# Two strided attention patterns taken as two lanes of tokens

## The reference

```python
for g, (window, dil) in enumerate(((128, 1), (512, 4), (2048, 16))):
    q, k, v = qkv[:, :, g, 0], qkv[:, :, g, 1], qkv[:, :, g, 2]
    o, lam = band_attention(to_strided(q, dil), to_strided(k, dil), to_strided(v, dil), window // dil)
    outs.append(from_strided(o, dil)); lams.append(from_strided(lam, dil))
alpha = softmax(stack(lams), axis=0)
y = sum(alpha[..., None] * stack(outs), axis=0)      # then y @ w_out
```

## Time and profile before

| | |
|---|---|
| runs | 1695.08, 1688.87, 1686.69 us (median 1688.87) |
| the profiled execution, first to last instruction | 1693.3 us, 21693 instructions |
| TensorE busy | 1643.5 us (97%) |
| VectorE / ScalarE busy | 638.1 us (38%) / 452.3 us (27%) |
| chain that ended last | TensorE 76%, VectorE 12%, DMA 5%, ScalarE 4% of the span |
| mean granted TensorE clock | 0.990 of full speed |

### The profile page before, as it was taken

The page is one execution under the profiler, slowest core; times in us unless marked ns, Lnnn a source line. Parts: engine busy times, 40 slices in busy tenths (PEclk is TensorE's granted clock), DMA queues, the critical chain, the costliest instruction groups (busy, mean ns, idle before and its releaser), DMA issues.

```text
span 1693.3 us, 21693 instructions
## 1 busy us (share of the span) xinstructions
PE 1643.5 (97%) x8195; PEld 963.5 (57%) x8195; DVE 638.1 (38%) x1382; ACT 452.3 (27%) x1167; POOL 135.3 (8%) x280
## 2 busy tenths in 40 slices
PE   8999989999999999999999999989999999999997
PEld 7888777644344344435878868856743443444342
DVE  3689983422222222214033544554422222222223
ACT  3477761211111111112152242232311111111111
POOL 1223230100000000002001102310000000000000
PEclk9999999999999999999999999999999999999999
DMA  9557676599999999997436918576499999999994
GB/s 336 204 181 226 198 227 245 197 384 429 428 427 428 428 428 428 428 424 287 156 113 217 337 63 269 169 236 273 164 369 406 428 428 427 427 429 428 428 428 179
DMA packets 101672, 538.04 MB, mean 318 GB/s; under 512 B 7997, under 2 KB 32773, under 8 KB 76723
## 3 DMA queue, kind: packets, MB, share of 16 engines
q1 hardware_dynamic: 85910, 485.20, 70.9%
q0 software_dynamic: 15360, 51.30, 9.6%
q10 hardware_dynamic: 316, 0.37, 0.1%
HBM read 520.61 MB, written 16.42 MB: 317 GB/s over the span
## 4 chain that ended last, share of the span: by engine, by line
PE 76%; DVE 12%; DMA 5%; ACT 4%; issue 2%; SPq 0%; DVEq 0%; ACTq 0%
PE bank L968 24%; PE bank L980 12%; PE bank L1348 12%; PE bank L952 5%; DMA ring<-in_moe_w_gate_up 5%; PE bank L833 4%; PE bank L974 4%; PE bank L1273 3%; PE bank L1245 3%; DVE arena L2326 2%; PE bank L1539 2%; DVE arena L2175 1%; ACT arena L1872 1%; PE bank L994 1%; PE bank L1386 1%
## 5 line engine op out<-in xcount | busy, mean ns | idle before, releaser
L968 PE MATMUL bank<-ring,arena 128*64 128x512 f32 x1520 | 339.3, 597 | 5.7 <-DMA ring<-in_moe_w_gate_up 5.7
L1348 PE MATMUL bank<-hT,ring 128*128 128x264 f32 x1152 | 270.6, 391 | 0.0
L1348 PEld LDWEIGHTS bank<-hT,ring 128*128 128x128 f32 x1152 | 216.3, 191 | 43.9 <-issue 9.1
L968 PEld LDWEIGHTS bank<-ring,arena 128*64 128x64 f32 x1520 | 113.1, 138 | 219.4 <-issue 219.1
L2175 DVE TENSOR_TENSOR arena<-arena,bank 128x512 f32<-128x512 f32 x32 | 34.3, 1072 | 395.5 <-ACT arena L1654 395.5
L980 PE MATMUL bank<-ring,arena 128*64 128x512 f32 x768 | 170.1, 595 | 1.6 <-DVE arena L2096 1.6
L974 PE MATMUL bank<-arena 128*128 128x512 f32 x256 | 127.0, 618 | 1.6 <-ACT arena L1664 1.6
L1654 ACT ACTIVATE arena<-bank 128x512 f32<-128x512 f32 x32 | 19.1, 597 | 394.9 <-PE bank L968 394.9
L2122 DVE SCALAR_TENSOR_TENSOR arena<-arena 128x1024 f32<-128x1024 f32 x32 | 41.1, 1285 | 213.3 <-ACT arena L1664 213.3
L968 PE MATMUL bank<-arena 128*64 128x512 f32 x512 | 112.6, 592 | 0.0
L833 PE MATMUL bank<-ident,arena 128*128 128x128 f32 (+5 forms) x609 | 98.8, 275 | 13.6 <-ACT arena L1880 6.8
(11 more groups left out here) (333 smaller groups left out, 1779.3 us busy)
## 6 DMA issues: line engine op xcount, KB each, us to landing
ring<-in_moe_w_gate_up SPq DMA_DIRECT2D x94, 2048.0 KB, 18.4
ring<-in_moe_w_down SPq DMA_DIRECT2D x48, 2048.0 KB, 22.7
arena<-in_moe_w_gate_up SPq DMA_DIRECT2D x32, 2048.0 KB, 17.6
ring<-in_attn_qkv SPq DMA_DIRECT2D x18, 2048.0 KB, 11.8
arena<-in_moe_w_down SPq DMA_DIRECT2D x16, 2048.0 KB, 22.2
ring<-in_ssm_in_proj SPq DMA_DIRECT2D x10, 2048.0 KB, 14.3
out<-arena POOLq DMA_DIRECT2D x24, 512.0 KB, 4.1
arena<-in_cache_kv_w POOLq DMA_DIRECT2D x20, 512.0 KB, 7.7
```

Of the source, the lines that this page charges most:

```text
L968: mm = pe.matmul(bank[j][e * SLOTS:(e + 1) * SLOTS, :], Xg[:, 4 * half + k, 2 * (p % 2) + e, :], gate_rows(2 * half + e, p, k, first)[:, j ...
L1348: mm = pe.matmul(bank[i % 2][:, 0:T], wv[:, k, (i % 4) * P:(i % 4 + 1) * P], hT[:, k, :], start=(k == 0), stop=(k == DT - 1))
```

## The change

The keys and queries of patterns 1 and 2 are stored with the even tokens first and the odd ones behind (two lanes of 128). As an even token never sees an odd one, a head needs two blocks of 128 queries by 128 keys, 256 columns of scores instead of 384. ScalarE writes the lanes as it copies the projected tiles: it reads the bank at a stride of two elements, and copies the 8 sample columns by an instruction of their own. The four probability blocks of a pair of heads fit into bank 4 and are turned in one run (`turn_both`), behind `rows_job`, and copied by one instruction (`copy_both`). The running maxima and sums of pattern 0 stand in token order; once, after the third tile of pattern 1, TensorE multiplies them with columns 0, 2, .. and 1, 3, .. of the identity (`sums_to_lanes`) and VectorE copies them back in lanes. `taken_up` reads and writes yT, which stays in token order, at a stride of two. The rows of keys and values for output lie in lanes too, and the store sends them to tokens 2p and 2p + 1. The special place of one turn in pattern 2 (in front of `lagging(2, 2)`) goes. Pattern 0 is as before, apart from names.

```diff
+LANES = 2
...
                 link(pool.memset(mask[:, g, :], 0.0))
-                for c0, c1, base in ((0, P, 0), (P, 3 * P, P)):
+                for c0, c1, base in ((0, P, 0), (P, 3 * P, P)) if g == 0 else ((0, P, 0),):
                     v_ = mask[:, g, c0:c1]
                     link(pool.affine_select(out=v_, in_=v_, compare_op=ALU.is_ge, fill=NEG, base=base,
                                             pattern=[[-1, c1 - c0]], channel_multiplier=1))
                     if g == 0:
                         link(pool.affine_select(out=v_, in_=v_, compare_op=ALU.is_ge, fill=NEG, base=P - base,
                                                 pattern=[[1, c1 - c0]], channel_multiplier=-1))
-            pool.iota(pT[:, 0, 0, :, :].rearrange("p a b -> p (a b)").bitcast(I32), [[-1, 3 * P]], base=4 * P,
+            pool.iota(pT[:, 0, 0, 0, :].bitcast(I32), [[-1, P]], base=4 * P,
...
                 lo = 1 if g == 0 else 0
-                rows = kv_p[g][0, 0].rearrange("(c p) w h d -> p c w (h d)", p=P)
+                rows = kv_p[g][0, 0].rearrange("(p c) w h d -> p c w (h d)" if g else "(c p) w h d -> p c w (h d)", p=P)
...
                     pe.wait_ge(y_cp, t - 4)
+                if g:
+                    for c in range(LANES):
+                        for h in range(2):
+                            r = slice(h * HD, (h + 1) * HD)
+                            mm = pe.matmul(bank[2 + h][:, c * P:(c + 1) * P], qT[r, t, c * P:(c + 1) * P], kT[r, t, c * P:(c + 1) * P],
+                                           start=True, stop=True)
+                            if c:
+                                mm.then_inc(h_s, 1)
+                    return
...
 
-            def turn(g, t, h):
+            def turn(t, h):
+                pe.wait_ge(h_e, 4 * (t + 1))
+                if t or h:
+                    pe.wait_ge(h_c, 2 * t + h)
+                for j in range(3):
+                    mm = transpose(bank[4][:, j * P:(j + 1) * P], sm[:, t % 2, h, j * P:(j + 1) * P])
+                mm.then_inc(h_t, 1)
+
+            def turn_both(g, t):
+
                 n = DT * g + t
                 if g < 2:
                     pe.wait_ge(h_e, 4 * (n + 1))
                 else:
                     pe.wait_ge(h_n, t + 1)
-                if n or h:
-                    pe.wait_ge(h_c, 2 * n + h)
-                for j in range(3):
-                    mm = transpose(bank[4][:, j * P:(j + 1) * P], sm[:, t % 2, h, j * P:(j + 1) * P])
-                    if n == NGRP * DT - 1 and h == 0 and j == 0:
-                        mm.then_inc(moes[1].gu, 1)
-                mm.then_inc(h_t, 1)
+                if n == DT:
+                    pe.wait_ge(s_dt, 4)
+                pe.wait_ge(h_c, 2 * n)
+                for h in range(2):
+                    for c in range(LANES):
+                        mm = transpose(bank[4][:, (LANES * h + c) * P:(LANES * h + c + 1) * P],
+                                       sm[:, t % 2, h, c * P:(c + 1) * P])
+                        if n == NGRP * DT - 1 and h == 0 and c == 0:
+                            mm.then_inc(moes[1].gu, 1)
+                mm.then_inc(h_t, 2)
+
+            def sums_to_lanes():
+
+                pe.wait_ge(h_o, DT)
+                pe.wait_ge(h_c, 2 * DT)
+                for c in range(LANES):
+                    for j in range(2):
+                        mm = pe.matmul(bank[4][j * HD:(j + 1) * HD, 3 * P + 2 * AH * c:3 * P + 2 * AH * (c + 1)],
+                                       ident[:, c:P:LANES], O_st[:, 0:3:2, j, :], start=True, stop=True)
+                mm.then_inc(s_dtp, 1)
...
                         k = (2 * t + h) * HD
-                        mm = pe.matmul(bank[6][h * HD:(h + 1) * HD, c * P:TP], KV[:, c, k:k + HD],
-                                       pT[:, t % 2, h, 2 * c:2 + c, :].rearrange("p a b -> p (a b)"),
-                                       start=(c == 0), stop=(c == 1))
+                        out, probs = bank[6][h * HD:(h + 1) * HD, :], pT[:, t % 2, h, :, :]
+                        if g:
+                            mm = pe.matmul(out[:, c * P:(c + 1) * P], KV[:, c, k:k + HD], probs[:, c, :],
+                                           start=True, stop=True)
+                        else:
+                            mm = pe.matmul(out[:, c * P:TP], KV[:, c, k:k + HD],
+                                           probs[:, 2 * c:2 + c, :].rearrange("p a b -> p (a b)"),
+                                           start=(c == 0), stop=(c == 1))
...
 
-                if 1 <= s <= DT:
-                    turn(g, s - 1, 0)
+                if g == 0 and 1 <= s <= DT:
+                    turn(s - 1, 0)
                 if s <= DT:
                     rows_job(g, 8 + s)
+                if g and 1 <= s <= DT:
+                    turn_both(g, s - 1)
...
                     values(g, s - 2)
-                if 1 <= s <= DT and (g < NGRP - 1 or s > 1):
-                    turn(g, s - 1, 1)
+                if g == 0 and 1 <= s <= DT:
+                    turn(s - 1, 1)
 
             for g in range(NGRP):
                 for t in range(DT):
                     qkv_tile(24 * g + t)
                     if g and t < 2:
                         lagging(g - 1, DT + t)
+                    elif g == 1 and t == 2:
+                        sums_to_lanes()
...
                     qkv_tile(24 * g + 2 * DT + t)
-                    if g == NGRP - 1 and t == 2:
-                        turn(g, 0, 1)
...
                     dst = vT[:, t % 2, :]
-                act.activation(dst, bank[n % 2][:, 0:T], ACT.Copy).then_inc(q_e, 1)
+                if g:
+                    act.activation(dst[:, TP:T], bank[n % 2][:, TP:T], ACT.Copy)
+                    act.activation(dst[:, 0:TP].rearrange("p (c i) -> p c i", c=LANES),
+                                   bank[n % 2][:, 0:TP].rearrange("p (i c) -> p c i", c=LANES), ACT.Copy).then_inc(q_e, 1)
+                else:
+                    act.activation(dst, bank[n % 2][:, 0:T], ACT.Copy).then_inc(q_e, 1)
...
                 for h in range(2):
-                    for i, (c0, c1) in enumerate(((0, P), (P, 3 * P))):
+                    for i, (c0, c1) in enumerate(((0, P), (P, 2 * P if g else 3 * P))):
                         k = 2 * t + h
                         act.activation(sm[:, t % 2, h, c0:c1], sm[:, t % 2, h, c0:c1], ACT.Exp,
                                        bias=Mn[:, i, k:k + 1], accum_out=rs[:, i, k:k + 1]).then_inc(h_e, 1)
 
-            def copy_probs(g, t, h):
-                n = DT * g + t
-                act.wait_ge(h_t, 2 * n + h + 1)
-                if n >= 2:
-                    act.wait_ge(h_v, n - 1)
+            def copy_probs(t, h):
+                act.wait_ge(h_t, 2 * t + h + 1)
+                if t >= 2:
+                    act.wait_ge(h_v, t - 1)
                 act.activation(pT[:, t % 2, h, :, :].rearrange("p a b -> p (a b)"), bank[4][:, 0:3 * P],
                                ACT.Copy).then_inc(h_c, 1)
 
+            def copy_both(g, t):
+                n = DT * g + t
+                act.wait_ge(h_t, 2 * n + 2)
+                act.wait_ge(h_v, n - 1)
+                act.activation(pT[:, t % 2, :, 0:LANES, :].rearrange("p h c q -> p h (c q)"),
+                               bank[4][:, :].rearrange("p (h q) -> p h q", h=2), ACT.Copy).then_inc(h_c, 2)
+
             n_keys = sum(KEYS) + NGRP
 
             def lagging(g, s):
-                if 1 <= s <= DT:
-                    copy_probs(g, s - 1, 0)
+                if g == 0 and 1 <= s <= DT:
+                    copy_probs(s - 1, 0)
                 if s <= DT:
                     copy_rows(g, 8 + s)
+                if g and 1 <= s <= DT:
+                    copy_both(g, s - 1)
...
             v.tensor_copy(mask[:, 0, 0:1], mask[:, 0, 0:1]).then_inc(a_mv, 1)
-            dist = pT[:, 0, 0, :, :].rearrange("p a b -> p (a b)")
-            rest = pT[:, 0, 1, :, :].rearrange("p a b -> p (a b)")
+            dist, rest, apart = pT[:, 0, 0, 0, :], pT[:, 0, 1, 0, :], sm[:, 0, 0, 0:P]
             for g in range(1, NGRP):
-                link(v.tensor_scalar(rest.bitcast(I32), dist.bitcast(I32), PATTERNS[g][1] - 1, None, ALU.bitwise_and))
-                link(v.tensor_copy(sm[:, 0, 0, :], rest.bitcast(I32)))
-                link(v.tensor_scalar(sm[:, 0, 0, :], sm[:, 0, 0, :], 0.0, NEG, ALU.not_equal, ALU.mult))
-                v.tensor_tensor(mask[:, g, :], mask[:, g, :], sm[:, 0, 0, :], ALU.min).then_inc(a_mv, 1)
+                link(v.tensor_scalar(rest.bitcast(I32), dist.bitcast(I32), PATTERNS[g][1] // LANES - 1, None,
+                                     ALU.bitwise_and))
+                link(v.tensor_copy(apart, rest.bitcast(I32)))
+                link(v.tensor_scalar(apart, apart, 0.0, NEG, ALU.not_equal, ALU.mult))
+                v.tensor_tensor(mask[:, g, 0:P], mask[:, g, 0:P], apart, ALU.min).then_inc(a_mv, 1)
...
```

(44 more changed lines are left out.)

## The result

The changed kernel takes 1666.31 us (median of 4 runs, 1664.96 to 1668.82) against 1688.98 (1686.69 to 1695.08): ratio 0.9847, 95% interval 0.9817 to 0.9877, or 22.7 us less (the interval: 21 to 31 us). The forecast was 1667 and 22.4. The profiled execution took 1665.94 us, its span is 1663.9, so about 2.0 lie around a span; the one of before fits 1695.08 in the same way.

A forecast was written before the change was run, and what follows sets the result against it. TensorE's work and a round through three engines were taken to bound patterns 1 and 2. Pattern 1's 11.6 plus pattern 2's 11.4 less 0.6 gave 22.4 us, from 1688.87 to 1666.5, say 1667; own range 1661 to 1673, overall 1658 to 1679.

The forecast's parts named there:

- What bounds it: Patterns 1 and 2, value steps: TensorE work nearly all the time, 9.9 us idle; pattern 1's round through three engines.
- Scores and values: Each step's score and value matmuls: scores 0.65 instead of 0.86 us (-0.21), values 0.49 instead of 0.75 (-0.26).
- Turns: Transposes of each step: six in 0.78 us, 0.31 us less than the 1.09 before.
- The step and what is late next: Pattern 1's full step: TensorE work 6.91 becomes 6.13 us and bounds it; mask ends at 3.7, ScalarE's copies at 6.8.
- Copies: ScalarE's 48 tile copies, read at stride two: no cost to the total, each some 0.05 us longer.
- Taking up: VectorE's output step, yT at stride two: taken as nothing; upper end twice the time, 0.84 us a step.
- Turning the sums: Eight small matmuls after pattern 1's third tile: cost 0.6 us, between 0.49 and 1.0.
- The low clock: Term: 1.4 us removed after pattern 1's starting wait. Rival: TensorE stays at 1.2 GHz in pattern 1, 1715 us, chance 0.03.
- Whether the rest takes it on: Kernel after attention, up to the last experts: it shifts as a whole, so the gain is kept.
- VectorE late in pattern 2: Rival: strided taking up at twice its time, 0.84 us in steps 4 to 7 and first ones; 1671 us, chance 0.12.
- Only the columns count: Rival: idle time and low clock stay, only work shrinks, 11.7 us less; 1677 us, chance 0.13.
- The stream: Rival: the weights' stream sets the last experts' start, so nothing is left of the gain; 1688 us, chance 0.05.

The follow-up runs named there:

- e2: Kernel before, blocks unchanged, but pattern 1's six transposes per pair of heads in one run; 1689.84 us, ratio 0.9986 to the kernel before.
- e8: Kernel before, no edit, profiled a second time; pattern 1's part 119.82 us instead of 120.91, pattern 2's 79.86.
- e1: Changed kernel, but in patterns 1 and 2 each head's blocks are turned in a separate run again; 1676.23 us, ratio 0.9896 to the kernel before.
- e5: Changed kernel, but ScalarE copies projected tiles of patterns 1 and 2 by one plain instruction, without lane order; 1665.78 us, ratio 0.9859 to before.
- e4: Changed kernel plus two more 256-element VectorE instructions in every taking up of patterns 1 and 2; 1673.31 us, ratio 0.9885 to the kernel before.
- e3: Changed kernel, but the odd lane's scores computed against both lanes' keys, 256 columns instead of 128; 1672.12 us, ratio 0.9885 to the kernel before.
- e9: The kernel before with pattern 1's six transposes in one run, profiled a second time; pattern 1's part 114.53 us, pattern 2's 80.95.

## Why the prediction was right, point by point

- *What bounds it.* The round between the two heads, through three engines: e2 shortens it alone, with the same columns, and gets 6.4 us in pattern 1 (5.3 against e8's profile). Shown. What the prediction did not say is that the narrower blocks alone would have removed the wait in the steady steps too (e1).
- *Scores and values.* 0.65 us was taken and measured, -0.21. Values: 0.54 with scores behind them; at the old width and with scores behind, in e2, 984.44 - 983.69 = 0.75; so -0.21 and not -0.26.
- *Turns.* Six transposes 0.75 us for 1.09: -0.34, taken -0.31.
- *The step and what is late next.* 6.08 us, 6.13 was forecast: 0.83 less work than 6.91, as 0.21 + 0.34 + 0.28, because the 6.91 counted the values up to their modelled end (0.82). VectorE's mask ended at 3.7 us by the forecast; by the timeline 978.25 - 974.66 = 3.6. ScalarE's last copy 6.8, measured 981.2 - 974.66 = 6.5.
- *Copies.* Nothing, by e5. The strided copy of 256 elements takes 377 ns in the median, no more than L1903's plain one of the same size (380): the 0.05 us read from the earlier trace rows at stride four weren't there at stride two (L1633 also scales each row, so that reading mixed two things). With the instruction for the eight columns a tile's copy takes 979.99 to 980.42, 0.43 us, against 0.39 for L1831 before. The price that the prediction drew for the strided read from the Trainium skill, page "SBUF — State Buffer", section "Door 1: The DMA port swizzle (why `[64,N]` ≈ `[32,N]`)", did not show; what stands there of PSUM is said of matmuls.
- *Taking up.* 0.42 us an instruction, as before; the rule of the Trainium skill, page "SBUF — State Buffer", section "Door 1: The DMA port swizzle (why `[64,N]` ≈ `[32,N]`)", on 16-byte lines, by which the upper end fell away, agrees (422 against 420 and 421 ns). Had the upper end held, e4 shows the price: 0.9 us in each of steps 4 to 6 of pattern 2, and some in step 2 and the tail.
- *Turning the sums.* 0.6 us was taken; its matmuls took 909.96 - 909.60 = 0.36, below the lower end of 0.49; they have 32 columns and L1414's have 128. The stretch is 0.6 us longer all the same. The other 0.2 lies in the projected tiles that these matmuls part: the seven tiles around them took 3.76 + 21.56 = 25.32 us, and 25.12 in one piece before.
- *Sums.* Pattern 1, counted to pattern 2's first scores: 11.6 forecast, 11.5 measured. Pattern 2: 11.4, and 11.8 with another 0.2 behind the output projection's start; steps 0 to 2 gave 22.52 - 17.28 = 5.2 where 4.6 was forecast, so the 0.3 us of idling kept there did not stay, and as much again came besides; step 3 gave 0.8 for 0.7, steps 4 to 6 3.8 for 3.7, step 7 and the tail 2.1 for 2.4. In steps 4 to 6 it forecast "near 10.1" and got 9.98.
- *The low clock.* 1.4 us was booked as removed. e8, without it, has a part shorter by 1.1, so it cost 1.1 in the one execution and nothing in the other. The term was read from one execution of something that changes from one to the next. (the earlier trace rows also begins 0.6 us before the wait ends, so it is not the three us behind it.)
- *The closeness.* That 22.4 met 22.7 is partly luck. The interval reaches from 21 to 31 us, the touched parts give 22.7 us against the one profile of before and 21.6 against e8's, and terms that were off by up to 0.6 us in either direction cancelled in part.
- *Whether the rest takes it on.* From the output projection to the end nothing was given back (-1.4 us, inside the 4 us by which this stretch varies between profiles).
- *The rivals.* VectorE late in pattern 2 is not what happened, but the reason given for it was sound: e3 shows VectorE a hair behind TensorE. Only the columns count (the waits stay): refuted by the change, and e2 shows a gain without any column less. e1, the columns without the single run, keeps waits of 1.13 us in pattern 1's step 1 and 2.7 in pattern 2's step 2, and none in the steady steps (0.56 us more in pattern 2's tail): so the rival's waits hold mainly at the starts, and the columns do more than its sum gave them. The stream and the low clock: no sign; in the changed kernel's value steps the clock is 1.00, with runs of six transposes in each.

## What to carry to other kernels

Where a step goes through three engines, add up each engine's own work and the round between them separately; a stall of 0.4 us a step and 2 us at the start of a pattern was worth 5 to 6 us here. Merging two handovers into one removed it with no arithmetic saved; less arithmetic in every leg removed most of it too, so the two gains do not add up (6.4 and 9.8 us alone, 11.5 together). When an engine's wait is removed, look who is within 0.2 us of becoming the next: a doubled instruction there tells it at once. Judge by stretches of the trace that repeat to 0.1 us when whole executions scatter by several.

## What the runs showed of the hardware

- The granted clock after a wait of TensorE is not fixed by the wait: after the same 2.17 us it was 1.00 in e2 (and in both profiles of before) and 0.64 in e9, after 2.00 us 0.63 in before and after 2.05 us 1.00 in e8, after about 2.7 us in three pieces 0.50 to 0.53 in e1.
- ScalarE reading the bank at a stride of two float32 elements: 377 ns for 256, against 380 plain; VectorE with the output and one operand at stride two in the arena: 422 ns against 420 and 421 without the stride.
- The code ahead of the attention took 782.97 to 790.57 us over the twelve profiles, a spread of one third of the whole gain.
- Over thirteen runs of the kernel before, spans of 1683.5 to 1696.3 us went with mean granted clocks of 0.996 to 0.987: runs are compared best at the same clock.
